# Two transformer blocks on one core: the value products of block 2's three attention branches with the operands exchanged, heads in column halves

## The chip, the cores and the metric

One core of one Trainium2 chip runs the whole program. The metric is the time of one execution on the device in microseconds (us). Before the change three runs gave a median of 1591.19 us (1590.44 to 1591.41).

## The reference, cut to what matters

Batch 1, 256 tokens, width 1024, all in float32. Two different block types, each two layers deep, run one after the other. Only the second is changed:

```
for l in range(2):                                # second_block
    h = rms_norm_2(x, g_mix[l]);  proj = h @ w_in[l]
    y_a = mla_mixer(...)            # 8 heads, keys of 96, values of 64, full 256 x 256 softmax
    y_b = dilated_mixer(...)        # 4 head places x 3 dilation groups, values of 64; the three
                                    # groups are joined by a softmax over their log-sums
    y_c = neighbourhood_mixer(...)  # 8 heads, keys and values of 64, a window with a bias
    merged = gates0 * (y_a @ w_pa) + gates1 * (y_b @ w_pb) + gates2 * (y_c @ w_pc)
    x = x + merged @ w_o[l]
    h = rms_norm_2(x, g_ffn[l])
    x = x + (silu(h @ w1[l]) * (h @ w3[l])) @ w2[l]
```

Each branch is softmax(scores) times values for each head. In branch b the three groups of one head place share one softmax: the exponentials of all three, divided by their common sum, times their values, summed.

## The kernel before, in words

**Weights.** All weight matrices are cut into 252 pieces of up to 128 x 2048 floats, loaded in a fixed order into a ring of three buffers (`raw`), one DMA each from SyncE (SP). ScalarE rounds a piece to a high half (`split_high`, L895, `wh`), VectorE makes the low half (`split_low`, L1251, `wl`), and TensorE multiplies high by high, high by low and low by high (L404, L405, L406). A piece of full width is 24 such matmuls. Piece q+3 reuses the buffer of piece q. The pieces of a layer of block 2 are numbered 0 to 74; pieces 12, 13, 32 and 33 are half as wide as the others here (`NARROW`).

**Attention in steps.** Every engine has one list of instructions, written out by hand in this order, and all run in program order with semaphores between them. The attention of a layer is 24 steps, m = 0 to 23, beside pieces q = 11 + m: steps 0 to 7 are branch a, 8 to 15 branch b, 16 to 23 branch c (`step_kind`); within a branch four steps (j = 0 to 3) for each half t of the 256 queries. A step of a or c is two heads, a step of b is one head place with its three groups (768 keys). In each step TensorE does, after the matmuls of piece q: the value product of step m-1 (`weighted`, L796 or L802), the transposes of step m's probabilities (`probs_t`, by the helper at L442), and the scores of step m+1 (`scores`: L752 for a, L770 for b, L758 for c). The 128 queries' probabilities lie in `prob` with queries on partitions; their transpose `prob_t` has keys on partitions.

**The value product** takes 128 x 128 of `prob_t` as the stationary operand and 128 x 64 of the values as the moving one, so its output has queries on partitions and heads along the row. The exponentials of the softmax go in undivided. After the last step of a branch half, `output` (L1703) takes the reciprocal of the sums (L1710) and scales all heads at once from PSUM into `y` (L1711). The products with w_pb, w_pa and w_pc (pieces 32 and up) need y with its columns on partitions, so y is transposed on TensorE: branch b after step 17, branch a after steps 19 and 20, branch c in the middle of piece 35 (`branch_c_t`, L812). VectorE copies the transposes to `xf` (L1260), ScalarE makes the high half (L900), VectorE the low half (L1270).

**VectorE in a step**: copy the transposed probabilities out of PSUM (L1375), `output` where a half has ended, the row maxima of step m+1 (`row_max`; L1699, L1680 or L1694, then L1683 or L1700), and `split_low` of piece q+2 (L1770). From step 21 on a product of a gate (`merge`, L1722) comes first. **ScalarE in a step**: copies or gates out of PSUM (L929, L1177), `split_high` of piece q+3 (L1179), the exponentials of step m+1 (`softmax_exp`, L1142 or L1149). Half-array matmuls are already there in the scores of b and c, whose 64-row operands lie on partitions 0 to 63 or 64 to 127.

Of the kernel before, what the change touches and what calls it, by code (L numbers as in the profile page):

```python
# [76 lines left out]
    "tr_full": (24, 69), "tr_free": (24, 69), "xh_ready": (12, 19), "xl_ready": (12, 19),  # L77
# [9 lines left out]
    "s_full": (0, STEPS), "max_ready": (0, STEPS), "p_ready": (0, STEPS),  # L87
    "o_full": (0, 6), "o_free": (0, 6), "bias_in": (0, 256), "bias_ready": (0, 1), "merged_ready": (0, 2), "sum_ready": (0, 2),
    "dve_step": (52, 81), "act_step": (6, 0),
# [72 lines left out]
def block2_transposes():  # L162
    order = [("norm1", 4), ("a", 2), ("bq", 2), ("bqk", 1), ("aq", 4), ("bk", 2), ("ak", 1),
             ("bk_last", 1), ("ak_rest", 3)]
    for m in range(STEPS):
        order.append((("pt", m), 2 if 8 <= m < 16 else 1))
        order += {5: [("cq", 2)], 7: [("ck", 2)], 17: [("yb", 1)], 19: [("ya", 1)],
                  20: [("ya_last", 1)]}.get(m, [])
    order += [("yc", 2), ("m0", 2), ("m1", 2), ("norm2", 4)]
# [11 lines left out]
def build(nc, weights, x_in, gains1, gains2, g_mid, g_final, consts, masks, rpb, out):  # L181
    ctx = ExitStack()
    with ctx:
# [85 lines left out]


# [17 lines left out]
        s_full, max_ready, p_ready = S["s_full"], S["max_ready"], S["p_ready"]  # L288
        o_full, o_free = S["o_full"], S["o_free"]
# [58 lines left out]
        def step_kind(m):  # L348
            return "abc"[m // 8], (m % 8) // 4, m % 4

# [47 lines left out]
        def _(pe):  # L398
# [287 lines left out]
            for layer in range(DEPTH):  # L686
# [87 lines left out]
                def probs_t(m):  # L774
                    n = TR2["pt", m]
                    pe.wait_ge(*p_ready.by(L, m + 1))
# [5 lines left out]
                def weighted(m):  # L782

                    kind, t, j = step_kind(m)
                    pe.wait_ge(*tr_free.by(L, TR2["pt", m] + (2 if kind == "b" else 1)))
                    if j == 0:
                        pe.wait_ge(*o_free.by(L, max(0, m // 4 - 1)))
# [4 lines left out]
                    if kind == "b":  # L792
                        for b in range(6):
                            g, s = group_order(j)[b // 2], b % 2
                            h = 4 * g + j
                            mm = nc.tensor.matmul(o[:, j * 64:(j + 1) * 64], prob_t[:, b * P:(b + 1) * P],  # L796
                                                  bv[:, s, h * 64:(h + 1) * 64], start=b == 0, stop=b == 5)
                    else:
                        v = av if kind == "a" else cv
                        for b in range(4):  # L800
                            h, s = 2 * j + b // 2, b % 2
                            mm = nc.tensor.matmul(o[:, h * 64:(h + 1) * 64], prob_t[:, b * P:(b + 1) * P],  # L802
                                                  v[:, s, h * 64:(h + 1) * 64], start=s == 0, stop=s == 1)
# [7 lines left out]

                def branch_c_t():  # L812
                    pe.wait_ge(*o_free.by(L, 6))
                    for b in range(2):
# [1158 lines left out]
```

## Time and profile before

| what | value |
|---|---|
| median of three runs | 1591.19 us |
| the profiled execution, its own time | 1590.36 us |
| its span, first to last instruction | 1588.5 us |
| TensorE (PE) busy | 1567.9 us, 99% |
| PE weight loads (PEld) | 1304.7 us, 82% |
| VectorE (DVE) busy | 1037.2 us, 65% |
| ScalarE (ACT) busy | 769.4 us, 48% |
| GpSimd (POOL) busy | 39.8 us, 3% |

The busy times are unions of instruction spans. PE and PEld are two views of one engine: a matmul record and the weight load that goes with it. The ends of matmul records are modelled, so the distance from one start to the next tells more than a record's length. A f32 matmul that isn't a transpose leaves two records; a transpose or a matmul of the rounded halves leaves one. Block 2's first layer takes its 24 steps from about 702 to 878 us, its second some 474 us later.

### The profile page before, as it was taken

The numbers are of one execution on the slowest core, as the hardware profiler recorded it, in microseconds if no ns is written. First come the engines' busy times: TensorE is split into PE (matmuls) and PEld (weight loads), VectorE is DVE, ScalarE is ACT, GpSimd is POOL, SyncE is SP. The second block draws the span as 40 slices with busy tenths as digits, with TensorE's granted clock in tenths as the row PEclk, the third lists the DMA queues.
The fourth block names the chain that finished last, engine by engine and source line by source line (L and its number), as shares of the span: only waits on it lengthen the run. The fifth ranks groups of instructions, "written<-read, shape, count | busy, mean of one in ns | idle before, by whom it ended". The sixth has DMA issues, their size and how long they took to land.

```text
span 1588.5 us, 18655 instructions
## 1 busy us (share of the span) xinstructions
PE 1567.9 (99%) x7684; PEld 1304.7 (82%) x7684; DVE 1037.2 (65%) x1309; ACT 769.4 (48%) x891; POOL 39.8 (3%) x28
## 2 busy tenths in 40 slices
PE   7999999999999999999999999999999999999997
PEld 5888888888888888888888888888888888888886
DVE  4778656666875656965556875656865547776555
ACT  5655444456454444664445354444664444454443
POOL 0000000001000000000020100000000020100000
PEclk9999999999999999999999999999999999999999
DMA  8435555554355554443543455554543633555551
GB/s 298 175 109 189 196 188 191 178 186 159 108 210 186 185 188 150 165 157 133 143 137 131 163 209 185 185 189 152 185 136 131 160 132 123 186 204 193 183 195 55
DMA packets 54243, 267.23 MB, mean 168 GB/s; under 512 B 18704, under 2 KB 19344, under 8 KB 24208
## 3 DMA queue, kind: packets, MB, share of 16 engines
q1 hardware_dynamic: 40784, 262.02, 46.5%
q10 hardware_dynamic: 13376, 4.02, 1.9%
q8 instruction: 61, 1.00, 0.3%
q14 instruction: 22, 0.18, 0.0%
HBM read 264.98 MB, written 1.05 MB: 167 GB/s over the span
## 4 chain that ended last, share of the span: by engine, by line
PE 93%; DVE 4%; ACT 1%; DMA 1%; issue 1%; SPq 0%; DVEq 0%; ACTq 0%
PE psum L404 27%; PE psum L406 27%; PE psum L405 26%; PE psum L442 4%; PE psum L802 2%; PE psum L796 1%; PE psum L496 1%; PE psum L770 1%; DMA raw<-in_weights 1%; PE psum L752 1%; DVE wl L1251 1%; PE psum L758 1%; PE psum L614 0%; PE psum L598 0%; ACT wh L895 0%
## 5 line engine op out<-in xcount | busy, mean ns | idle before, releaser
L1251 DVE TENSOR_TENSOR wl<-raw,wh 128x2048 fp32r<-128x2048 f32 (+1 forms) x250 | 560.8, 2246 | 276.6 <-ACT wh L895 273.6
L895 ACT ACTIVATE wh<-raw 128x2048 fp32r<-128x2048 f32 (+1 forms) x250 | 467.1, 1873 | 398.1 <-PE psum L406 384.0
L404 PE MATMUL psum<-wh,xh 128*128 128x512 f32 (+1 forms) x1632 | 647.4, 397 | 8.8 <-ACT work L929 3.7
L406 PE MATMUL psum<-wh,xl 128*128 128x512 f32 (+1 forms) x1632 | 633.1, 388 | 0.0
L405 PE MATMUL psum<-wl,xh 128*128 128x512 f32 (+1 forms) x1632 | 632.0, 387 | 0.0
L404 PEld LDWEIGHTS psum<-wh,xh 128*128 128x128 f32 x1632 | 307.1, 188 | 78.0 <-issue 15.9
L406 PEld LDWEIGHTS psum<-wh,xl 128*128 128x128 f32 x1632 | 306.8, 188 | 63.2
L405 PEld LDWEIGHTS psum<-wl,xh 128*128 128x128 f32 x1632 | 307.5, 188 | 57.6
L1375 DVE COPY arena<-psum 128x512 f32<-128x512 f32 x100 | 61.9, 643 | 159.6 <-PE psum L442 144.9
L404 PE MATMUL psum<-wh,ah 128*128 128x512 f32 (+1 forms) x360 | 140.3, 390 | 0.0
L406 PE MATMUL psum<-wh,al 128*128 128x512 f32 (+1 forms) x360 | 139.4, 387 | 0.0
L405 PE MATMUL psum<-wl,ah 128*128 128x512 f32 (+1 forms) x360 | 139.3, 387 | 0.0
L943 ACT ACTIVATE work<-psum,rms 128x256 f32<-128x256 f32 x88 | 41.7, 474 | 127.0 <-PE psum L406 127.0
L404 PEld LDWEIGHTS psum<-wh,ah 128*128 128x128 f32 x360 | 67.6, 188 | 13.7 <-issue 0.7
L406 PEld LDWEIGHTS psum<-wh,al 128*128 128x128 f32 x360 | 67.6, 188 | 13.5
L405 PEld LDWEIGHTS psum<-wl,ah 128*128 128x128 f32 x360 | 67.6, 188 | 13.1
L900 ACT ACTIVATE xh<-xf 128x512 fp32r<-128x512 f32 x56 | 34.3, 630 | 75.2 <-DVE xf L1264 50.1
L1390 DVE TENSOR_SCALAR work<-psum,rms 128x256 f32<-128x256 f32 x88 | 42.1, 479 | 28.7 <-ACT work L943 28.7
L929 ACT ACTIVATE work<-psum,rms 128x512 f32<-128x512 f32 (+2 forms) x52 | 32.9, 638 | 41.0 <-PE psum L406 41.0
L1392 DVE SCALAR_TENSOR_TENSOR work<-psum,rms,work 128x256 f32<-128x256 f32 x88 | 42.6, 484 | 3.1
L1841 POOL TENSOR_TENSOR arena<-arena,col_mask 128x768 f32<-128x768 f32 x8 | 18.5, 2350 | 789.4 <-DMA arena<-in_rpb 789.4
L1270 DVE TENSOR_TENSOR xl<-xf,xh 128x512 fp32r<-128x512 f32 x56 | 36.5, 688 | 2.2
(159 smaller groups left out, 1054.7 us busy)
## 6 DMA issues: line engine op xcount, KB each, us to landing
raw<-in_weights SPq DMA_DIRECT2D x234, 1024.0 KB, 4.8
raw<-in_weights SPq DMA_DIRECT2D x10, 512.0 KB, 3.6
raw<-in_weights SPq DMA_DIRECT2D x4, 832.0 KB, 4.3
arena<-in_rpb ACTq DMA_DIRECT2D x32, 96.0 KB, 8.1
raw<-in_weights SPq DMA_DIRECT2D x8, 256.0 KB, 6.8
raw<-in_weights SPq DMA_DIRECT2D x2, 768.0 KB, 4.5
x<-in_x SPq DMA_DIRECT2D x4, 256.0 KB, 4.5
out<-arena SPq DMA_DIRECT2D x3, 256.0 KB, 3.1
```

What stands on the lines that cost most here:

```text
L404: nc.tensor.matmul(dst, lh, right(wh, slot), start=start, stop=False)
L405: nc.tensor.matmul(dst, lh, right(wl, slot), start=False, stop=False)
L406: return nc.tensor.matmul(dst, ll, right(wh, slot), start=False, stop=stop)
L442: mm = nc.tensor.transpose(psum[0:w, TR + n % 2, col:col + P], src, ident[:, :])
L895: nc.scalar.activation(wh[:, slot, 0:n], raw[:, slot, 0:n], ACT.Copy).then_inc(high_ready.sem, 1)
L900: nc.scalar.activation(dst, part(xf[:, n % 2, :], 0, nk, SEQ), ACT.Copy)\
L943: nc.scalar.activation(mlp_tanh[:, t, :], bank(PROJ + t)[:, 0:256], ACT.Tanh, scale=rms[:, 6 + t:7 + t]).then_inc(tanh_ready.sem, 1)
L1251: nc.vector.tensor_tensor(wl[:, slot, 0:n], raw[:, slot, 0:n], wh[:, slot, 0:n].bitcast(F32), ALU.subtract).then_inc(split_ready.sem, 1)
L1270: nc.vector.tensor_tensor(low, part(xf[:, n % 2, :], 0, nk, SEQ), high.bitcast(F32), ALU.subtract).then_inc(xl_ready.sem, 1)
L1375: nc.vector.tensor_copy(dst, src).then_inc(tr_free.sem, 1)
L1390: step.wait(L, nc.vector.tensor_scalar(mlp_gate[:, t, :], bank(PROJ + t)[:, 0:256], rms[:, t:t + 1], None, ALU.mult))
L1392: nc.vector.scalar_tensor_tensor(mlp_act[:, t, :], bank(PROJ + t)[:, 256:512], rms[:, 6 + t:7 + t], mlp_gate[:, t, :], ALU.mult, ALU.mult) ...
```

## The change

The value products of all three branches exchange their operands: the values (128 keys x 64) are stationary and the transposed probabilities (128 keys x 128 queries) move, so the output has the 64 value columns on partitions and queries along the row, which is y transposed. Two heads go to partitions 0 to 63 and 64 to 127 of the output, and their matmuls alternate. Branch b has one head place in a step, so the product of an even step is left to the odd one after it, where both steps' twelve products alternate; the odd step's transposed probabilities go to `xf` for that. Since a query's sum now lies along the row, the probabilities are divided before they are transposed (`unit_sums` on VectorE, with the new semaphore `unit_ready`, on which TensorE's transposes wait in place of `p_ready`). `output` only halves and copies, into `y_t`, views of `y` with columns on partitions. The transposes of y, their copies to `xf` and the waits on them go; high and low halves are made from `y_t`. The output of the first half of branch c goes to ScalarE at step 20. VectorE's splits change places: in steps 1, 21 and 22 `unit_sums` stands ahead of them, and splits 33 and 34 each come a step earlier. Left out of the diff below: numbers of semaphore counts (five transposes fewer, 18 more ordered VectorE steps in a layer), and the declaration of the semaphore.

```diff
@@ -267,6 +266,9 @@
+        y_flat = y[:, :, :].rearrange("p a b -> p (a b)")
+        y_t = {"a": part(y_flat, 0, 4, SEQ), "b": part(y_flat, 1024, 2, SEQ), "c": part(y_flat, 1536, 4, SEQ)}
+
...
@@ -347,6 +350,11 @@
             return "abc"[m // 8], (m % 8) // 4, m % 4
+
+        def transposed(m):
+
+            kind, _, j = step_kind(m)
+            return xf[:, :, :].rearrange("p a b -> p (a b)") if kind == "b" and j % 2 else prob_t
...
@@ -773,7 +781,7 @@
                     n = TR2["pt", m]
-                    pe.wait_ge(*p_ready.by(L, m + 1))
+                    pe.wait_ge(*unit_ready.by(L, m + 1))
                     blocks = 6 if step_kind(m)[0] == "b" else 4
...
@@ -782,8 +790,10 @@
                     kind, t, j = step_kind(m)
+                    if kind == "b" and j % 2 == 0:
+                        return
                     pe.wait_ge(*tr_free.by(L, TR2["pt", m] + (2 if kind == "b" else 1)))
-                    if j == 0:
+                    if j == (1 if kind == "b" else 0):
                         pe.wait_ge(*o_free.by(L, max(0, m // 4 - 1)))
...
@@ -791,16 +801,23 @@
                         for b in range(6):
-                            g, s = group_order(j)[b // 2], b % 2
-                            h = 4 * g + j
-                            mm = nc.tensor.matmul(o[:, j * 64:(j + 1) * 64], prob_t[:, b * P:(b + 1) * P],
-                                                  bv[:, s, h * 64:(h + 1) * 64], start=b == 0, stop=b == 5)
+                            for step in (m - 1, m):
+                                jj = step % 4
+                                g, s = group_order(jj)[b // 2], b % 2
+                                h = 4 * g + jj
+                                mm = nc.tensor.matmul(o[64 * (jj % 2):64 * (jj % 2) + 64, (j // 2) * P:(j // 2 + 1) * P],
+                                                      bv[:, s, h * 64:(h + 1) * 64],
+                                                      transposed(step)[:, b * P:(b + 1) * P],
+                                                      start=b == 0, stop=b == 5)
                     else:
                         v = av if kind == "a" else cv
-                        for b in range(4):
-                            h, s = 2 * j + b // 2, b % 2
-                            mm = nc.tensor.matmul(o[:, h * 64:(h + 1) * 64], prob_t[:, b * P:(b + 1) * P],
-                                                  v[:, s, h * 64:(h + 1) * 64], start=s == 0, stop=s == 1)
+                        for s in range(2):
+                            for hh in range(2):
+                                h = 2 * j + hh
+                                mm = nc.tensor.matmul(o[64 * hh:64 * hh + 64, j * P:(j + 1) * P],
+                                                      v[:, s, h * 64:(h + 1) * 64],
+                                                      prob_t[:, (2 * hh + s) * P:(2 * hh + s + 1) * P],
+                                                      start=s == 0, stop=s == 1)
                     if j == 3:
...
@@ -808,12 +825,6 @@
-
-                def branch_c_t():
-                    pe.wait_ge(*o_free.by(L, 6))
-                    for b in range(2):
-                        transpose_k(L, TR2["yc"] + b, lambda t, k: y[:, t, k * P:(k + 1) * P],
-                                    (6 + 2 * b, 7 + 2 * b))
...
@@ -853,15 +864,8 @@
                         staged_t(TR2["ck"], 0)
-                    if m == 17:
-                        pe.wait_ge(*o_free.by(L, 4))
-                        transpose_k(L, TR2["yb"], lambda t, k: y[:, t, k * P:(k + 1) * P], (4, 5))
-                    if m == 19:
-                        transpose_k(L, TR2["ya"], lambda t, k: y[:, t, k * P:(k + 1) * P], (0, 1))
-                    if m == 20:
-                        transpose_k(L, TR2["ya_last"], lambda t, k: y[:, t, k * P:(k + 1) * P], (2, 3))
                 weighted(STEPS - 1)
-                project(L, 35, 22, 0, between=branch_c_t)
+                project(L, 35, 22, 0)
...
@@ -869,7 +873,8 @@
-                project(L, 36, 23, 4, left_ready=9)
+                pe.wait_ge(*xl_ready.by(L, 11))
+                project(L, 36, 23, 4)
                 project(L, 37, 24, 4, between=lambda: merged(0))
...
@@ -1152,6 +1157,13 @@
+                def branch_c_high(t):
+
+                    act.wait_ge(*used(L, 31))
+                    act.wait_ge(*o_free.by(L, 5 + t))
+                    tq = slice(t * P, (t + 1) * P)
+                    nc.scalar.activation(xh[:, 4:8, tq], y_t["c"][:, :, tq], ACT.Copy).then_inc(xh_ready.sem, 1)
+
                 softmax_exp(0)
...
@@ -1177,14 +1189,24 @@
                     split_high(L, q + 3)
+                    if m == 20:
+                        act.wait_ge(*o_full.by(L, 5))
+                        nc.scalar.activation(y_t["c"][:, :, 0:P], part(bank(ACC + 2), 0, 4, P), ACT.Copy, scale=0.5)\
+                            .then_inc(o_free.sem, 1)
                     if m + 1 < STEPS:
...
                     if m == 17:
-                        operand_high(L, 6, TR2["yb"], dst=ah[:, 0:2, :])
+                        act.wait_ge(*used(L, 9))
+                        act.wait_ge(*o_free.by(L, 4))
+                        nc.scalar.activation(ah[:, 0:2, :], y_t["b"], ACT.Copy).then_inc(xh_ready.sem, 1)
                     if m == 19:
-                        operand_high(L, 7, TR2["ya"], dst=xh[:, 0:2, :])
-                    if m == 20:
-                        operand_high(L, 8, TR2["ya_last"], dst=xh[:, 2:4, :])
+                        act.wait_ge(*used(L, 30))
+                        act.wait_ge(*o_free.by(L, 2))
+                        for k in (0, 2):
+                            nc.scalar.activation(xh[:, k:k + 2, :], y_t["a"][:, k:k + 2, :], ACT.Copy)\
+                                .then_inc(xh_ready.sem, 1)
+                    if m == 21:
+                        branch_c_high(0)
                     if 8 <= m < 12:
...
@@ -1196,8 +1218,7 @@
                                 .then_inc(bias_in.sem, 16)
-                for b in range(2):
-                    operand_high(L, 9 + b, TR2["yc"] + b, dst=xh[:, 4 + 2 * b:6 + 2 * b, :])
+                branch_c_high(1)
                 split_high(L, 38)
...
@@ -1700,19 +1721,32 @@
+                def unit_sums(m):
+
+                    kind, t, j = step_kind(m)
+                    v.wait_ge(*p_ready.by(L, m + 1))
+                    heads = [prob] if kind == "b" else [prob[:, 0:SEQ], prob[:, SEQ:2 * SEQ]]
+                    at = 32 + 4 * t + j if kind == "b" else (0 if kind == "a" else 16) + 8 * t + 2 * j
+                    step.wait(L, nc.vector.reciprocal(rden[:, 0:len(heads)], den[:, at:at + len(heads)]))
+                    for hh, p in enumerate(heads):
+                        ins = nc.vector.tensor_scalar(p, p, rden[:, hh:hh + 1], None, ALU.mult)
+                    ins.then_inc(unit_ready.sem, 1)
+
                 def output(i):
...
                     kind, t = "abc"[i // 2], i % 2
-                    heads = 4 if kind == "b" else 8
-                    at = {"a": 0, "b": 32, "c": 16}[kind] + heads * t
-                    to = {"a": 0, "b": 512, "c": 768}[kind]
+                    k = 2 if kind == "b" else 4
                     v.wait_ge(*o_full.by(L, i + 1))
-                    step.wait(L, nc.vector.reciprocal(rden[:, 0:heads], den[:, at:at + heads]))
-                    nc.vector.scalar_tensor_tensor(
-                        y[:, t, to:to + heads * 64].rearrange("p (h e) -> p h e", e=64),
-                        part(bank(ACC + 2 + t), 0, heads, 64), 0.5,
-                        rden[:, 0:heads].unsqueeze(2).to_broadcast([P, heads, 64]), ALU.mult, ALU.mult)\
-                        .then_inc(o_free.sem, 1)
+                    nc.vector.tensor_scalar(y_t[kind][:, :, t * P:(t + 1) * P], part(bank(ACC + 2 + t), 0, k, P),
+                                            0.5, None, ALU.mult).then_inc(o_free.sem, 1)
+
+                def branch_low(n, src, high, low):
+                    v.wait_ge(*xh_ready.by(L, n + 1))
+                    nc.vector.tensor_tensor(low, src, high.bitcast(F32), ALU.subtract).then_inc(xl_ready.sem, 1)
+
+                def branch_c_low(t):
+                    tq = slice(t * P, (t + 1) * P)
+                    branch_low(9 + t, y_t["c"][:, :, tq], xh[:, 4:8, tq], xl[:, 4:8, tq])
...
@@ -1733,14 +1767,15 @@
+                unit_sums(0)
...
-                        copy_t(L, n, prob_t[:, 0:512], others=m == 0)
+                        copy_t(L, n, transposed(m)[:, 0:512], others=m == 0)
...
-                            copy_t(L, n + 1, prob_t[:, 512:768])
+                            copy_t(L, n + 1, transposed(m)[:, 512:768])
...
@@ -1752,7 +1787,7 @@
-                    if m >= 1 and (m - 1) % 4 == 3:
+                    if m >= 1 and (m - 1) % 4 == 3 and m != 20:
...
@@ -1761,25 +1796,23 @@
                                        c_t[:, first + 2 * b:first + 2 * b + 2, :])
+                        if m in (1, 21, 22):
+                            unit_sums(m + 1)
+                            if m != 21:
+                                split_low(L, 14 if m == 1 else 35)
+                        else:
+                            split_low(L, 34 if m == 20 else q + 2)
+                            unit_sums(m + 1)
                         if m == 17:
-                            operand_out(L, 6, TR2["yb"], None)
+                            branch_low(6, y_t["b"], ah[:, 0:2, :], al[:, 0:2, :])
                         if m == 19:
-                            operand_out(L, 7, TR2["ya"], None)
-                        if m == 20:
-                            operand_out(L, 8, TR2["ya_last"], None)
-                        split_low(L, q + 2)
-                        if m == 17:
-                            operand_low(L, 6, ah[:, 0:2, :], al[:, 0:2, :])
-                        if m == 19:
-                            operand_low(L, 7, xh[:, 0:2, :], xl[:, 0:2, :])
-                        if m == 20:
-                            operand_low(L, 8, xh[:, 2:4, :], xl[:, 2:4, :])
+                            for k in (0, 2):
+                                branch_low(7 + k // 2, y_t["a"][:, k:k + 2, :], xh[:, k:k + 2, :], xl[:, k:k + 2, :])
+                            split_low(L, 33)
                 output(5)
-
-                def branch_c():
-                    operand(L, 9, TR2["yc"], 4, None, 2)
-
-                merge(35, 0, 1, 23, between=branch_c)
+                branch_c_low(0)
+
+                merge(35, 0, 1, 23, between=lambda: branch_c_low(1))
                 split_low(L, 37)
```

## Rows read from the trace of the kernel before

**Rows 1.** The page: busy time by engine; shares of the chain that ended last.

```profile
PE 1567.9 (99%) x7684; PEld 1304.7 (82%) x7684; DVE 1037.2 (65%) x1309; ACT 769.4 (48%) x891; POOL 39.8 (3%) x28
...
PE 93%; DVE 4%; ACT 1%; DMA 1%; issue 1%; SPq 0%; DVEq 0%; ACTq 0%
```

**Rows 2.** Timeline of TensorE, last product and y's transposes: start, length, line, operands, count.

```profile
876.82 0.39 PE L406 MATMUL psum<-wh,xl 128*128 128x512 f32 x1
...
878.17 0.39 PE L405 MATMUL psum<-wl,xh 128*128 128x512 f32 x1
...
880.48 0.39 PE L406 MATMUL psum<-wh,xl 128*128 128x512 f32 x1
...
881.82 0.40 PE L405 MATMUL psum<-wl,xh 128*128 128x512 f32 x1
```

**Rows 3.** The same view in block 1: f32 streams with 128 and 256 moving columns.

```profile
87.79 0.39 PE L617 MATMUL psum<-arena 128*128 128x128 f32 x2
...
89.35 1.89 PE L598 MATMUL psum<-arena 128*128 128x256 f32 x8
91.08 1.05 PE L603 MATMUL psum<-arena 128*128 128x128 f32 x8
```

**Rows 4.** The same view around step 3, branch a.

```profile
725.12 0.39 PE L406 MATMUL psum<-wh,xl 128*128 128x512 f32 x1
...
727.72 0.40 PE L405 MATMUL psum<-wl,xh 128*128 128x512 f32 x1
```

**Rows 5.** The same view around step 10, branch b.

```profile
774.57 0.39 PE L406 MATMUL psum<-wh,xl 128*128 128x512 f32 x1
...
776.84 1.13 PE L770 MATMUL psum<-arena 64*128 64x256 f32 x6
...
778.23 0.39 PE L405 MATMUL psum<-wl,xh 128*128 128x512 f32 x1
```

**Rows 6.** The same view around step 18, branch c.

```profile
842.22 0.39 PE L406 MATMUL psum<-wh,xl 128*128 128x512 f32 x1
...
843.82 0.70 PE L758 MATMUL psum<-arena 64*128 64x256 f32 x4
...
844.79 0.39 PE L405 MATMUL psum<-wl,xh 128*128 128x512 f32 x1
```

**Rows 7.** Groups by line and shape: busy us, mean ns, idle before.

```profile
L1817 DVE TENSOR_SCALAR arena<-arena,rms 128x512 f32<-128x512 f32 x3 | 1.3, 483 | 0.0
...
L1658 DVE TENSOR_SCALAR work<-work,rms 128x256 f32<-128x256 f32 x4 | 1.2, 351 | 0.1
```

**Rows 8.** Timelines of VectorE and TensorE, step 8 to 9.

```profile
762.22 2.28 DVE L1251 TENSOR_TENSOR wl<-raw,wh 128x2048 fp32r<-128x2048 f32 x1
...
765.90 0.39 PE L406 MATMUL psum<-wh,xl 128*128 128x512 f32 x1
```

**Rows 9.** Timelines of VectorE, ScalarE and TensorE, steps 1 and 2.

```profile
708.24 2.28 DVE L1251 TENSOR_TENSOR wl<-raw,wh 128x2048 fp32r<-128x2048 f32 x1
...
709.18 0.20 ACT L1149 ACTIVATION_READ_ACCUMULATOR arena<-psum,smax 128x1 f32 x1
...
712.50 0.40 PE L405 MATMUL psum<-wl,xh 128*128 128x512 f32 x1
```

**Rows 10.** The same views, steps 20 and 21.

```profile
858.85 0.61 PE L442 MATMUL psum<-ident,arena 128*128 128x128 f32 x4
...
858.80 1.90 ACT L895 ACTIVATE wh<-raw 128x2048 fp32r<-128x2048 f32 x1
...
860.33 0.69 DVE L1711 SCALAR_TENSOR_TENSOR y<-psum,rden 128x512 f32<-128x512 f32 x1
...
861.82 0.69 DVE L1260 COPY xf<-psum 128x512 f32<-128x512 f32 x1
...
864.12 0.61 PE L442 MATMUL psum<-ident,arena 128*128 128x128 f32 x4
```

More of the change, by code:

```diff
@@ L76 @@
     "acc_full": (5, 5), "x_ready": (8, 8),
-    "tr_full": (24, 69), "tr_free": (24, 69), "xh_ready": (12, 19), "xl_ready": (12, 19),
+    "tr_full": (24, 64), "tr_free": (24, 64), "xh_ready": (12, 19), "xl_ready": (12, 19),
     "sumsq_ready": (4, 3), "var_ready": (4, 3), "root_ready": (4, 3), "rms_ready": (2, 3),
@@ L86 @@
     "aq_ready": (0, 1), "ak_ready": (0, 1),
-    "s_full": (0, STEPS), "max_ready": (0, STEPS), "p_ready": (0, STEPS),
+    "s_full": (0, STEPS), "max_ready": (0, STEPS), "p_ready": (0, STEPS), "unit_ready": (0, STEPS),
     "o_full": (0, 6), "o_free": (0, 6), "bias_in": (0, 256), "bias_ready": (0, 1), "merged_ready": (0, 2), "sum_ready": (0, 2),
-    "dve_step": (52, 81), "act_step": (6, 0),
+    "dve_step": (52, 99), "act_step": (6, 0),
 }
@@ L166, in block2_transposes @@
         order.append((("pt", m), 2 if 8 <= m < 16 else 1))
-        order += {5: [("cq", 2)], 7: [("ck", 2)], 17: [("yb", 1)], 19: [("ya", 1)],
-                  20: [("ya_last", 1)]}.get(m, [])
-    order += [("yc", 2), ("m0", 2), ("m1", 2), ("norm2", 4)]
+        order += {5: [("cq", 2)], 7: [("ck", 2)]}.get(m, [])
+    order += [("m0", 2), ("m1", 2), ("norm2", 4)]
     at, where = 0, {}
@@ L288, in build @@
         s_full, max_ready, p_ready = S["s_full"], S["max_ready"], S["p_ready"]
+        unit_ready = S["unit_ready"]
         o_full, o_free = S["o_full"], S["o_free"]
```

## The prediction

> **What bounds the kernel now.** I read the page's busy line and its chain first: TensorE has work for 1567.9 of 1588.5 us, and 93% of the chain that ended last is TensorE [rows 1]. So an edit in block 2's attention is worth what it changes in the stream of matrix records, plus any moment in which that stream newly waits. The view for both is the timeline of TensorE around one of the 24 steps, with those of VectorE and ScalarE beside it.
>
> How I price a step: take the start of the last L406 record of a weight piece and the start of the first L405 record after the step, and subtract two normal spacings of 0.23 us (that L406's own and the L404's between them). What is left is what the step inserts. Done on the lone last product of the layer, eight records insert 878.17 - 876.82 = 1.35 less 0.46, so 0.89 us, 0.111 a record; eight transposes of y insert 881.82 - 880.48 = 1.34 less 0.46, 0.88 us, 0.11 each [rows 2]. A f32 matmul leaves two records, so a step of branch a or c has 8 product records and one of b has 12. Inside a stream of f32 records with 128 moving columns the spacing is (89.35 - 87.79) / 14 = 0.111 us, and with 256 columns (91.08 - 89.35) / 8 = 0.216 [rows 3]. So a product with 64 moving columns costs the same as one with 128: turning it round (v stationary with 64 columns, probabilities moving with 128) does not by itself cost more.
>
> A step of branch a inserts 2.60 - 0.46 = 2.14 us [rows 4]; 8 + 4 records at 0.11 and the four 256-column score records at 0.216 give 2.18. Nothing is left over. A step of b inserts 3.66 - 0.46 = 3.20 [rows 5]: 12 + 6 records are 1.98; its six score records work on half the rows each, and two pairs of them run beside each other, so they take four places, 0.86; 0.36 is left. A step of c inserts 2.57 - 0.46 = 2.11 [rows 6]: 1.32 for twelve, 0.43 for two places of paired records, and again 0.36 is left. So going into half-array matmuls and back costs about 0.36 us a time, and pairs on two halves do run at the same time: four score records in two places.
> The Trainium skill says the same of the price: "TensorEngine Tiling (Array Packing)", Key Properties, has it that changing the tiling mode drains the engine. By that rule the column halves of the change pay it too; the 96-row scores of branch a don't, and rows 4 agree.
>
> **The change, part by part** (both layers together; 32 steps of a and c, 8 pairs of b steps).
> 1. *Products of a and c.* Before: 8 x 0.11 = 0.88 us. After: the two heads go to column halves, four places of 0.112 if they run together, plus a way in and out: 0.45 + 0.36 = 0.81. Gain 0.07 x 32 = 2.2 us. No row shows column halves. Bounds of one place: 0.108 (the stream of 128 columns, half of 0.216) and 0.223 (one after the other). Bounds of the way in and out: 0 (as in branch a) to about 0.6 if leaving fp32r work for column halves costs more than rows 5 and 6 show. I take 0.112 and 0.36, since the row halves in the same kernel, same data type, are the nearest rows.
> 2. *Products of b.* Before: 24 x 0.11 = 2.64 us for two steps. After: one way in and out for both and twelve places: 1.34 + 0.36 = 1.70. Gain 0.94 x 8 = 7.5 us.
> 3. *Transposes of y.* 20 a layer go (yb 4, ya 4, ya_last 4, yc 8): 40 x 0.11 = 4.4 us, all in TensorE's stream. The copies behind them go from VectorE too.
> 4. *unit_sums.* VectorE now divides the probabilities before they are transposed: a reciprocal and two 256-column scales, or one of 768. Rows: 0.351 us for 256 columns and 0.483 for 512, SBUF to SBUF with a scalar from a column [rows 7]; the same line to 768 gives 0.62. With 0.2 for the reciprocal and the wait, 0.85 us a step, some 40 us in all on an engine that is busy 1037 of 1588 us. It is on TensorE's path only where it ends after TensorE is ready to transpose. In a full step of b it starts at the end of the split, 762.22 + 2.28 = 764.50, and ends at 765.35, while the piece ends at 765.90 + 0.23 = 766.13 [rows 8]: hidden, with 0.8 us to spare, and that is the tightest kind (an odd b step, with no product ahead of the transposes). Full steps of a and c have the products to spare as well. If the cover went, each step would pay its lateness once.
>  Two places are tighter. (i) Step m=1 puts unit_sums(2) before split_low(14): ScalarE's exponentials end at 709.38, the scales at 710.2, and the split, 2.28 us, at 712.45; TensorE wanted piece 14 at 712.50 - 0.23 = 712.27, and now 0.14 earlier after two cheaper products [rows 9]. It waits about 0.4 us. (ii) The narrow pieces 32 and 33. The transposes of step 20 now start 0.5 us earlier, 858.35 instead of 858.85. The row maxima of step 21 ended 861.82 - 858.85 = 2.97 us after them, with the output of branch c (0.9 us) between; that output goes to ScalarE, so it is 2.1 and VectorE is free at 860.5 (ScalarE's split of piece 34 ends at 860.2 at the latest, so that is no later). Then split_low(34), 2.28, and unit_sums(21), 0.85: 863.6. TensorE wants to transpose at 864.12 - 0.9 = 863.2, having lost two groups of transposes and some of two products [rows 10]: 0.4 us late. Steps 22 and 23 come out level by the same counting (VectorE: two gate products, copy, maxima, scales; ScalarE: exponentials), within 0.2 us. Together about 1.0 us a layer, 2.0 in all; bounds 0 and 6 (each of steps 21, 22, 23 late by 0.6 as well).
> 5. *Moved.* Output 4 to ScalarE before its exponentials of step 21 (0.7 us, inside the 2 us in which it waits for the maxima); the high and low halves of y come straight from SBUF instead of over xf, earlier than before; splits 33 and 34 run a step earlier, so SP's loads of pieces 36 and 37 start earlier, split 35 and with it the load of 38 about a microsecond later with several to spare. Branch c's last operand is still made during piece 35, 5.5 us long, and needs about 3. I cost all of it at nothing, for that cover.
>
> Sum: -2.2 - 7.5 - 4.4 + 2.0 = -12.1. The profiled execution took 1590.36 us, so 1578.3; the median of the runs, 1591.19, is 0.83 above it, so 1579.1.
>
> A rule of the skill speaks against this: "TensorE: Matmul & The Clock Gate", Part 3, says that a weight load overlaps a running matmul only where the row groups differ, and column halves share all rows. In this trace full-array products reload 128 rows and columns every 0.111 us beside the stream, so loads do hide behind matmuls of the same rows; the rule is therefore not taken as it stands, but it is what the next two rivals would be.
>
> **Rivals.**
> - *A, the halves take turns* (slower). Each column half has its load and its stream one after the other, 0.111 a record. Then a and c: 0.89 + 0.36 = 1.25, +0.37 x 32 = +11.8; b: 2.66 + 0.36 = 3.02, +0.38 x 8 = +3.0; transposes -4.4; waits about +1 since TensorE comes later. +11.4: 1602.6. It decides from a place of 0.17 us upward. For: no row shows column halves, and the spacing of 0.111 at 64 as at 128 moving columns says that loads are what bounds these records. Against: the loads get half as wide, and row halves run in pairs.
> - *B, half hidden*: a pair takes 0.167, one 64-column load (half of 0.111) beyond the stream. a and c: 0.67 + 0.36 = 1.03, +0.15 x 32 = +4.8; b: 2.00 + 0.36 = 2.36, -0.28 x 8 = -2.2; -4.4 + 2.0: +0.2, 1591.4, no change.
> - *C, VectorE late*: halves overlap, but the scales end late in steps 1 and 21 to 23, 6 us in all: 1583.1. For: steps 22 and 23 are within 0.2 us; against: all other steps have 0.8 us or more.
> - *D, no price for column halves*: 0.36 x 40 = 14.4 more, of which some 3 turn into waits for VectorE: 1567.7. For: branch a's 96 rows pay none; against: both kinds of half-array matmul here do.
>
> **How the numbers follow.** My forecast 0.50, A 0.18, B 0.14, C 0.12, D 0.06. A measurement of this kernel can tell 0.2%, 3.2 us, from no change. Forecast, C and D are faster, 0.68; B splits into 0.05 faster, 0.05 same, 0.04 slower; A is slower. So 0.73, 0.05, 0.22. The range leaves out A and D: 1571 (a cheaper way in and out, no new waits) to 1594 (B with its own error, or a way in and out of 0.7 us instead of 0.36, which alone would add 14 us).
>
> **What would show it.** In the profile after: product records that start in pairs a few ns apart, and an insert of about 2.1 us for an a step with 0.8 of it for the products (A would show records 0.111 apart; B pairs 0.167 apart); an idle of TensorE's weight queue of about 0.2 us at the way in and again at the way out; one long group of 24 records in every second b step, 1.3 us; no transposes of y in block 2; waits of TensorE on VectorE's scales at steps 1 and 21 of each layer, under 0.6 us, and none in the other steps. The forecast is wrong if column halves don't pair, or if the scales are waited for in every step.

## The result and the profile after

Four runs of the changed kernel gave a median of 1579.91 us (1579.04 to 1580.84) against 1591.30 for the kernel before on the same chip: a ratio of 0.9928, 95% interval 0.9916 to 0.9940. The forecast was 1579.1 us. The profiled execution took 1579.04 us, 11.3 less than the one before, where the sum said 12.1.

The page of the changed kernel, lines that answer to [rows 1]:

```profile
PE 1555.5 (99%) x7644; PEld 1272.9 (81%) x7644; DVE 1068.8 (68%) x1413; ACT 769.0 (49%) x893; POOL 40.1 (3%) x28
...
PE 89%; DVE 7%; ACT 2%; DMA 1%; issue 1%; SPq 0%; DVEq 0%; ACTq 0%
```

Forty matmul records fewer (the transposes of y), 104 VectorE instructions more, and TensorE's share of the chain down from 93% to 89%: VectorE now ends some waits. In the changed kernel L412, L413 and L414 are the former L404 to L406, L450 the former L442; the products are L808 (branch b) and L817 (a and c), the scales of `unit_sums` L1732 (the reciprocal before it L1730), the split L1272, `output` L1740, the low halves of y L1745, GpSimd's sum of gates L1881.

The timeline of TensorE around step 3, branch a, which answers to [rows 4], and the same stretch of its weight queue (PEld):

```profile
725.72 0.39 PE L414 MATMUL psum<-wh,xl 128*128 128x512 f32 x1
726.04 0.66 PE L817 MATMUL psum<-arena 128*64 128x128 f32 x8
726.63 0.66 PE L450 MATMUL psum<-ident,arena 128*128 128x128 f32 x4
...
728.22 0.39 PE L413 MATMUL psum<-wl,xh 128*128 128x512 f32 x1
```

```profile
726.04 0.42 PEld L817 LDWEIGHTS psum<-arena 128*64 128x64 f32 x8 [0.35 <-issue]
726.62 0.42 PEld L450 LDWEIGHTS psum<-ident,arena 128*128 128x128 f32 x4 [0.17 <-issue]
```

By the measure of the prediction the step inserts 728.22 - 725.72 - 0.46 = 2.04 us instead of 2.14. The weight queue is idle before the first load of the column halves and again before the first full-array load behind them: that is the way in and out. The product of the pair of b steps 8 and 9, which TensorE makes in its step 10, in the first of the two views; it answers to [rows 5]. Here operands tell the halves apart, `arena` for the even step's probabilities and `xf` for the odd one's:

```profile
773.33 0.39 PE L414 MATMUL psum<-wh,xl 128*128 128x512 f32 x1
773.64 0.32 PE L808 MATMUL psum<-arena 128*64 128x128 f32 x1
773.65 0.32 PE L808 MATMUL psum<-xf,arena 128*64 128x128 f32 x1
773.80 0.27 PE L808 MATMUL psum<-arena 128*64 128x128 f32 x1
773.81 0.27 PE L808 MATMUL psum<-xf,arena 128*64 128x128 f32 x1
773.91 0.27 PE L808 MATMUL psum<-arena 128*64 128x128 f32 x1
...
774.90 0.27 PE L808 MATMUL psum<-xf,arena 128*64 128x128 f32 x1
775.11 0.87 PE L450 MATMUL psum<-ident,arena 128*128 128x128 f32 x6
```

The records start in twos, 0.01 us apart, and the twos follow every 0.11 us. Twelve places for 24 records.

In this attention TensorE now waits at three places of each layer: at piece 14 (VectorE's split, late behind the scales), behind the product of step 20 (VectorE's scales L1732 in front of the transposes) and at piece 36. The timeline of TensorE there, first layer:

```profile
712.89 0.50 PE L412 MATMUL psum<-wh,xh 128*128 128x512 f32 x1 [0.18 <-DVE wl L1272]
...
857.99 0.66 PE L817 MATMUL psum<-arena 128*64 128x128 f32 x8
859.11 0.66 PE L450 MATMUL psum<-ident,arena 128*128 128x128 f32 x4 [0.47 <-DVE arena L1732]
...
878.86 0.50 PE L412 MATMUL psum<-wh,xh 128*128 128x512 f32 x1 [0.52 <-DVE xl L1745]
```

The bracket at piece 14 understates that wait: the step before it inserts 2.38 us, and 1.94 where the scales are left out (below). The third wait wasn't forecast. VectorE's timeline before it, then GpSimd's:

```profile
874.49 0.69 DVE L1740 TENSOR_SCALAR y<-psum 128x512 f32<-128x512 f32 x1
875.09 2.52 DVE L1745 TENSOR_TENSOR xl<-y,xh 128x512 fp32r<-128x512 f32 x1
877.53 0.67 DVE L1756 SCALAR_TENSOR_TENSOR work<-work,psum 128x512 f32<-128x512 f32 x1
878.13 0.68 DVE L1745 TENSOR_TENSOR xl<-y,xh 128x512 fp32r<-128x512 f32 x1
```

```profile
874.65 2.40 POOL L1881 TENSOR_TENSOR work<-work 128x1024 f32<-128x1024 f32 x1 [67.22 <-DVE work L1756]
```

The same subtraction takes 0.68 us the second time and 2.52 the first, while GpSimd's sum of gates runs from 874.65 to 877.05. The instruction ends 0.56 us after GpSimd does, as if it had only begun then. TensorE starts piece 36 about 0.8 us late for it, in each layer.

GpSimd also works beside the scales once in each layer, in its additions on `arena` at branch b. VectorE's timeline and GpSimd's, first layer:

```profile
801.92 3.82 DVE L1272 TENSOR_TENSOR wl<-raw,wh 128x2048 fp32r<-128x2048 f32 x1
...
805.85 2.00 DVE L1732 TENSOR_SCALAR arena<-arena,rden 128x768 f32<-128x768 f32 x1
```

```profile
798.15 9.28 POOL L1874 TENSOR_TENSOR arena<-arena,col_mask 128x768 f32<-128x768 f32 x4 [406.64 <-DMA arena<-in_rpb]
```

The split takes 3.82 us instead of 2.28 there and the scale 2.00 instead of 0.62, although the scale reads only one large operand. The cover holds even so: that pair of b steps inserts 0.04 us more than the others.

### The profile page after: what moved, and what is told of

It is laid out like the page before. It is cut to its first block, busy times and chain, and to the rows that moved or that the text cites. A ratio compares the mean times of both kernels' runs of the same rounds, so it can differ in the third digit from the quotient of the medians.

```text
span 1577.3 us, 18675 instructions
## 1 busy us (share of the span) xinstructions
PE 1555.5 (99%) x7644; PEld 1272.9 (81%) x7644; DVE 1068.8 (68%) x1413; ACT 769.0 (49%) x893; POOL 40.1 (3%) x28
## 4 chain that ended last, share of the span: by engine, by line
PE 89%; DVE 7%; ACT 2%; DMA 1%; issue 1%; SPq 0%; DVEq 0%; ACTq 0%
PE psum L412 26%; PE psum L414 26%; PE psum L413 26%; PE psum L450 4%; DVE wl L1272 2%; PE psum L504 1%; PE psum L778 1%; DMA raw<-in_weights 1%; PE psum L817 1%; PE psum L760 1%; PE psum L808 1%; DVE work L1756 1%; ACT wh L900 0%; PE psum L622 0%; PE psum L606 0%
## 5 line engine op out<-in xcount | busy, mean ns | idle before, releaser
L1272 DVE TENSOR_TENSOR wl<-raw,wh 128x2048 fp32r<-128x2048 f32 (+1 forms) x250 | 561.8, 2250 | 277.1 <-ACT wh L900 274.1
L412 PE MATMUL psum<-wh,xh 128*128 128x512 f32 (+1 forms) x1632 | 647.8, 397 | 9.0 <-ACT work L934 3.0
L414 PE MATMUL psum<-wh,xl 128*128 128x512 f32 (+1 forms) x1632 | 633.3, 388 | 0.0
L413 PE MATMUL psum<-wl,xh 128*128 128x512 f32 (+1 forms) x1632 | 632.5, 388 | 0.0
L412 PEld LDWEIGHTS psum<-wh,xh 128*128 128x128 f32 x1632 | 307.3, 188 | 81.7 <-issue 16.8
L414 PEld LDWEIGHTS psum<-wh,xl 128*128 128x128 f32 x1632 | 307.2, 188 | 63.2
L413 PEld LDWEIGHTS psum<-wl,xh 128*128 128x128 f32 x1632 | 307.8, 189 | 57.4
L412 PE MATMUL psum<-wh,ah 128*128 128x512 f32 (+1 forms) x360 | 140.4, 390 | 0.0
L414 PE MATMUL psum<-wh,al 128*128 128x512 f32 (+1 forms) x360 | 139.3, 387 | 0.0
L413 PE MATMUL psum<-wl,ah 128*128 128x512 f32 (+1 forms) x360 | 139.2, 387 | 0.0
L1396 DVE COPY arena<-psum 128x512 f32<-128x512 f32 x84 | 53.7, 661 | 94.7 <-PE psum L450 83.9
L412 PEld LDWEIGHTS psum<-wh,ah 128*128 128x128 f32 x360 | 67.6, 188 | 14.4 <-issue 1.3
L414 PEld LDWEIGHTS psum<-wh,al 128*128 128x128 f32 x360 | 67.6, 188 | 13.5
L413 PEld LDWEIGHTS psum<-wl,ah 128*128 128x128 f32 x360 | 67.6, 188 | 13.1
L905 ACT ACTIVATE xh<-xf 128x512 fp32r<-128x512 f32 x48 | 29.4, 631 | 69.4 <-DVE xf L1285 50.6
L450 PEld LDWEIGHTS psum<-ident,work 128*128 128x128 f32 (+1 forms) x252 | 29.1, 136 | 8.1 <-issue 2.0
```

Source lines behind the costliest of these rows:

```text
L412: nc.tensor.matmul(dst, lh, right(wh, slot), start=start, stop=False)
L413: nc.tensor.matmul(dst, lh, right(wl, slot), start=False, stop=False)
L414: return nc.tensor.matmul(dst, ll, right(wh, slot), start=False, stop=stop)
L450: mm = nc.tensor.transpose(psum[0:w, TR + n % 2, col:col + P], src, ident[:, :])
L905: nc.scalar.activation(dst, part(xf[:, n % 2, :], 0, nk, SEQ), ACT.Copy)\
L1272: nc.vector.tensor_tensor(wl[:, slot, 0:n], raw[:, slot, 0:n], wh[:, slot, 0:n].bitcast(F32), ALU.subtract).then_inc(split_ready.sem, 1)
```

## The experiments

Each is an edit of the changed kernel. Ratios are to the kernel before on the same chip as the run (1592.13 us for the first four edits, 1592.06 for the others). Beside the time, the table gives a length that leaves out the noise of block 1: in the profiled execution, from the first score record of branch a in block 2 to the last matmul record (before: 693.21 to 1580.00). It rests on one execution each: in some of them a wait of TensorE for one of ScalarE's gates (0.17 to 0.53 us) turns up that others don't have, so a difference of half a microsecond has to be traced to its rows.

| kernel | median us (runs) | ratio to before, 95% interval | that length, us |
|---|---|---|---|
| before | 1591.3 (4) | | 886.8 |
| the change | 1579.91 (4) | 0.9928, 0.9916 to 0.9940 | 875.0 |
| halves in turn | 1587.85 (10) | 0.9974, 0.9964 to 0.9984 | 882.8 |
| full array in a and c | 1584.00 (4) | 0.9950, 0.9935 to 0.9965 | 878.9 |
| no scales | 1577.43 (4) | 0.9907, 0.9892 to 0.9922 | 872.0 |
| sum later | 1578.24 (4) | 0.9916, 0.9902 to 0.9931 | 873.7 |
| pairs in all branches | 1576.98 (4) | 0.9905, 0.9889 to 0.9922 | 871.9 |
| pairs, and sum later | 1575.84 (4) | 0.9902, 0.9887 to 0.9916 | 871.6 |
| b in blocks of 2 | 1580.98 (1) | | 875.7 |
| b in blocks of 3 | 1581.96 (1) | | 877.2 |

**Halves in turn.**

```diff
-                        for b in range(6):
-                            for step in (m - 1, m):
+                        for step in (m - 1, m):
+                            for b in range(6):
...
-                        for s in range(2):
-                            for hh in range(2):
+                        for hh in range(2):
+                            for s in range(2):
```

> The changed kernel, except that the matmuls of one column half all come before those of the other (branches a and c: head by head; branch b: step by step), so neighbours in the stream use the same half. Same matmuls, same number of ways in and out. Theory (column halves gain because neighbouring matmuls on different halves run side by side): a record takes 0.111 us instead of half a place, so a and c steps insert 2.05 + 0.45 us and a pair of b steps 3.52 + 1.3; 32 x 0.45 + 8 x 1.3 = +25 us against the changed kernel, so about 1604. Rival (the gain comes from stationary operands of half the width, which load faster, or the engine pairs them in any order): the product stays at 0.6 to 0.7 us and the time at 1580.

Measured: 7.8 us slower in the trace, not 25. A step of a inserts 2.05 us (2.04 before the edit), a step of c 2.00 as before: there the order doesn't matter. A pair of b steps inserts 4.44 instead of 3.52, and 8 x 0.92 = 7.4 is nearly all of the loss. TensorE's timeline of a pair of b steps:

```profile
773.90 1.20 PE L808 MATMUL psum<-arena 128*64 128x128 f32 x9
774.83 0.32 PE L808 MATMUL psum<-xf,arena 128*64 128x128 f32 x1
774.93 0.27 PE L808 MATMUL psum<-arena 128*64 128x128 f32 x1
774.99 0.27 PE L808 MATMUL psum<-xf,arena 128*64 128x128 f32 x1
775.04 0.27 PE L808 MATMUL psum<-arena 128*64 128x128 f32 x1
775.10 0.27 PE L808 MATMUL psum<-xf,arena 128*64 128x128 f32 x1
775.15 0.27 PE L808 MATMUL psum<-arena 128*64 128x128 f32 x1
775.21 1.15 PE L808 MATMUL psum<-xf,arena 128*64 128x128 f32 x9
```

Neither theory holds as it was put. One half alone runs a record in 0.109 us, against 0.111 for the full array, so half-width weights make next to nothing faster; but neighbours need not alternate either. The second half's first record starts beside the ninth of twelve, with three of the first half's records still ahead of it. So TensorE starts work of an idle half out of the program's order, some four records early, and four records of a head in a and c are within that reach. The Trainium skill, "TensorE: Matmul & The Clock Gate", Part 3, says that matmuls start strictly in program order; these rows contradict it. New theory: a look-ahead of four records. Two runs put it to the test.

**Blocks of 2 and of 3 matmuls in branch b.** The edit for blocks of 2; the other has 3 in place of each 2.

```diff
-                        for b in range(6):
-                            for step in (m - 1, m):
+                        for b0 in range(0, 6, 2):
+                            for step, b in [(step, b) for step in (m - 1, m) for b in range(b0, b0 + 2)]:
```

> The changed kernel with branch b's products in blocks: two matmuls (four records) of one step's half, then two of the other's, and so on. Theory (TensorE starts a record of the idle half when the running half is at most four records ahead of it in order, as the run with the halves in turn showed: the second half began beside the ninth of twelve): full overlap as when alternating, a pair of b steps inserts 3.5 us. Rival (only neighbours overlap): 3.5 + about 0.6 to 1.1.

> The same in blocks of three matmuls (six records). Theory (look-ahead of four records): the idle half starts beside the third record of a block, two places lost in all, a pair of b steps inserts 3.5 + 0.22 = 3.7 us. Rival (look-ahead of eight records or of time, not of order): 3.5.

Each was run once, so the times don't rank them; the inserts of all eight pairs in a trace can be compared. Measured: 3.57 us a pair in blocks of 2 (in two places more, 3.64 and 3.78), 3.79 in blocks of 3, against 3.52. In blocks of 2 the second half starts 0.01 us after the first. In blocks of 3, TensorE's timeline shows the second half starting beside the third record, 774.35 + 2 x 0.11 and a little:

```profile
774.35 0.54 PE L808 MATMUL psum<-arena 128*64 128x128 f32 x3
774.62 0.32 PE L808 MATMUL psum<-xf,arena 128*64 128x128 f32 x1
...
775.60 0.27 PE L808 MATMUL psum<-arena 128*64 128x128 f32 x1
775.66 0.49 PE L808 MATMUL psum<-xf,arena 128*64 128x128 f32 x3
```

The start is where the new theory puts it, to 0.05 us, and the inserts are 0.07 us over what it said (3.5 and 3.72). Whether the reach is four records or a number of instructions that holds four of them, these runs don't tell.

**Full array in a and c.**

```diff
-                                mm = nc.tensor.matmul(o[64 * hh:64 * hh + 64, j * P:(j + 1) * P],
-                                                      v[:, s, h * 64:(h + 1) * 64],
+                                mm = nc.tensor.matmul(o[:, j * P:(j + 1) * P],
+                                                      v[:, s, 2 * j * 64:(2 * j + 2) * 64],
...
-                                                      start=s == 0, stop=s == 1)
+                                                      start=(s, hh) == (0, 0), stop=(s, hh) == (1, 1))
```

> The changed kernel, except that in branches a and c both heads' values are stationary together (128 columns, full array) for each head's probabilities, and all four matmuls of a step add into one output: the heads are mixed, so the outputs of a and c are left wrong. Eight records of the full array, no way in or out of column halves. Theory (a way in and out costs 0.36 us and eats nearly all that the pairing gives in a step of two heads): 0.88 us for a product instead of 0.77 measured in the changed kernel, +0.11 x 32 = +3.5 us, about 1583.5, and no idle of the weight queue around the product. Rival (the idle shown there is no cost, only how records are drawn): 0.88 against 0.45, +0.43 x 32 = +14 us, 1594.

Measured: +3.9 us in the trace. TensorE's timeline around step 3 of branch a:

```profile
725.97 0.39 PE L414 MATMUL psum<-wh,xl 128*128 128x512 f32 x1
726.20 1.05 PE L817 MATMUL psum<-arena 128*128 128x128 f32 x8
...
728.62 0.40 PE L413 MATMUL psum<-wl,xh 128*128 128x512 f32 x1
```

The weight queue has no idle around it. The lone last product inserts 0.89 us, and 0.79 in the changed kernel. Pairs take 4 x 0.109 = 0.44 of that, so the way in and out is 0.35. The rival is out: it would have shown +14. A step of a inserts 2.65 - 0.46 = 2.19 us here against 2.04 with column halves and 2.14 in the kernel before, a step of c 2.16 against 2.00 and 2.11. So in branches a and c the column halves gain about 0.15 us a step over the full array, and turning the product round without them costs 0.05. Where TensorE waits for VectorE anyway (piece 14, step 21, half of the wait at piece 36), the longer product costs nothing, which is why the whole is 3.9 and not 32 x 0.15 = 4.8.

**No scales.**

```diff
-                    step.wait(L, nc.vector.reciprocal(rden[:, 0:len(heads)], den[:, at:at + len(heads)]))
-                    for hh, p in enumerate(heads):
-                        ins = nc.vector.tensor_scalar(p, p, rden[:, hh:hh + 1], None, ALU.mult)
-                    ins.then_inc(unit_ready.sem, 1)
+                    nc.vector.reciprocal(rden[:, 0:len(heads)], den[:, at:at + len(heads)])\
+                        .then_inc(unit_ready.sem, 1)
```

> The changed kernel without the division: VectorE only takes the reciprocal and signals, the probabilities are left undivided, so the output is wrong. Theory (some 42 us of new work on VectorE costs only where TensorE waits for it, 0.5 us at step 21 and 0.4 at piece 14 of each layer): -1.9 us, 1578. Rival 1 (VectorE's load also delays the splits and loads over the whole stretch, or slows ScalarE): more than -4 us. Rival 2 (the waits are of other origin): 0.

Measured: -3.0 us in the trace. The step before piece 14 inserts 1.94 instead of 2.38 us, the one with step 21's transposes 2.00 instead of 2.53: together 0.97 a layer. The wait of 0.8 us at piece 36, which the expectation left out, is gone as well: without the scales VectorE ends the last low half 6.0 us after the last product starts, not 6.8, though the long subtraction is still there (2.50 us). That would be -3.5; one pair of b steps in the first layer gives 0.6 back, where TensorE waits 0.53 us for a gate of ScalarE (L1189), at 795.01. So 32.4 us of scales on VectorE cost 2 to 3 us of time.

**Sum later.**

```diff
+                    if n == 0:
+                        pool.wait_ge(*xl_ready.by(L, 11))
```

> The changed kernel, except that GpSimd's first sum of gates waits until the last low half of branch c is done (xl_ready 11) before it starts. Theory (VectorE's subtraction for branch c's first low half took 2.5 us instead of 0.69 because GpSimd was adding at the same time, and that is why TensorE waits 1.0 us at piece 36 of each layer): the subtraction back at 0.69, the wait gone, -2.0 us, about 1578. Rival (it was slow for another reason, ScalarE's copy beside it): the subtraction stays above 2 us and the time at 1580; or the collision moves to the split that follows and delays piece 38, then +0 to +1.

Measured: -1.3 us in the trace. The group of L1745 `xl<-y,xh` runs from 679 to 687 ns, none at 2.5 us, and no wait at piece 36 is left. VectorE's and GpSimd's timelines:

```profile
875.28 0.68 DVE L1745 TENSOR_TENSOR xl<-y,xh 128x512 fp32r<-128x512 f32 x1
...
879.18 2.68 DVE L1272 TENSOR_TENSOR wl<-raw,wh 128x2048 fp32r<-128x2048 f32 x1
```

```profile
877.31 2.40 POOL L1883 TENSOR_TENSOR work<-work 128x1024 f32<-128x1024 f32 x1 [69.78 <-DVE xl L1745]
```

The sum now meets a gate product with one operand in PSUM at 878.58, which takes 0.69 us, and only the end of it meets a split, which takes 2.68 instead of 2.28. The gain is 1.3 us instead of the 2.0 expected, since the wait was 0.8 a layer and not 1.0, and the transposes that follow piece 36 insert 0.97 us instead of 0.88. By the medians alone it couldn't be told from the changed kernel; the rows show it. The Trainium skill, "SBUF — State Buffer", "Who interferes with whom", says that GpSimd and a VectorE operation with two SBUF inputs lock each other out for a whole instruction; the 2.52 us agree, and so does the untouched PSUM operand.

**Pairs in all branches.** `weighted` returns for every even j, `transposed` gives `xf` for every odd one, the waits for free buffers move to the odd steps, and the product of a and c loops over both steps. The second kernel has the edit of *sum later* besides.

```diff
-                        for s in range(2):
-                            for hh in range(2):
-                                h = 2 * j + hh
...
+                        for step in (m - 1, m):
+                            jj = step % 4
+                            for s in range(2):
+                                for hh in range(2):
+                                    h = 2 * jj + hh
```

> The changed kernel with branches a and c done as branch b: the product of an even step waits for the odd one (its probabilities in the other buffer), so two steps share one way in and out of the column halves. Theory (that way costs 0.33 us, measured as 0.77 us for eight records in pairs, less four places of 0.109): 16 pairs x 0.33 = -5.3 us, the wait for piece 14 gone, -0.9, but the transposes of odd steps follow straight on a piece and wait for VectorE's scales at steps 1, 21 and 23, some +0.25, +0.6 and +0.35 a layer: together -3.7 against the changed kernel, about 1576. Rival (the waits take all of it, since VectorE's order was set for single steps): 1580 or more, with over 2.5 us of waits a layer on the scales.

> The previous kernel, with GpSimd's first sum of gates held back until branch c's last low half is done. Theory (the two edits don't meet): the wait of 1.0 us at piece 36 of each layer goes here too, another -2.0 us, about 1574.3 and the fastest of all. Rival (the later product of steps 22 and 23 makes output and low halves the last again): no difference to the kernel without it.

Measured: -3.1 and -3.4 us in the trace. Two steps of a insert 1.31 + 2.48 = 3.79 us instead of 4.08: 0.3 for each pair saved, where 0.33 was priced. But step 21's transposes follow straight on piece 32 now and wait for the scales. TensorE's timeline of the first, then VectorE's:

```profile
857.35 0.39 PE L414 MATMUL psum<-wh,al 128*128 128x512 f32 x1
858.80 0.66 PE L450 MATMUL psum<-ident,arena 128*128 128x128 f32 x4 [1.06 <-DVE arena L1734]
```

```profile
855.73 2.28 DVE L1274 TENSOR_TENSOR wl<-raw,wh 128x2048 fp32r<-128x2048 f32 x1
857.93 0.16 DVE L1732 RECIPROCAL rden<-den 128x2 f32<-128x2 f32 x1
858.13 0.62 DVE L1734 TENSOR_SCALAR arena<-arena,rden 128x256 f32<-128x256 f32 x2
```

That is 1.3 us a layer where 0.6 on top of 0.5 was expected. The sum held back removes the wait at piece 36 here too, but its expectation missed: -0.3 us against the kernel without it, not -2.0. With pairs everywhere that wait was down to 0.5 us a layer. Of the 1.0 so gained, 0.2 is lost at the transposes behind piece 36, and 0.5 in one wait for a gate of ScalarE (0.49 us at 776.52) that the other trace doesn't have.

This last kernel has the lowest median, 1575.84 us, 16.2 below the kernel before on its chip. Its interval only touches that of the change, so it is faster than the change by the traces and the medians together; from the one without the later sum no run tells it apart.

## Why the prediction was right

By the steps of the prediction, all from the traces.

1. *Products of a and c*: forecast -2.2; a step of a fell from 2.14 to 2.04 us, one of c from 2.11 to 2.00, so about 0.105 x 32 = -3.4. This term was mis-sized. A step without a product inserts 1.31 us (pairs in all branches), so the product of a fell from 0.83 to 0.73, not from 0.88 to 0.81. The old one was cheaper than counted where transposes follow it: "does not by itself cost more" holds for the lone product only, elsewhere turning costs 0.05, as the full-array run showed. The new one was cheaper still: a place is 0.109 and the way in and out 0.29 in a step (0.35 at the lone product), where I took 0.112 and 0.36.
2. *Products of b*: forecast -7.5; two steps inserted 3.20 each, 6.40 us, before and 1.91 + 3.52 = 5.43 after: -0.97 x 8 = -7.8.
3. *Transposes of y*: forecast -4.4; three groups of 0.39 and one of 0.88 a layer, -4.1.
4. *Waits on the scales*: forecast +2.0; 0.44 at piece 14 and 0.53 at step 21 a layer, +1.9, both at the places named. Scales took 0.351 and, undisturbed, 0.62 us, the numbers taken.
5. *Moved work*: forecast 0; this is the step that failed, in its sentence that branch c's last operand "needs about 3" of piece 35's 5.5 us. From the output's start to the end of the last low half it took 878.81 - 874.49 = 4.3 us, since GpSimd's sum stood beside the first subtraction, and VectorE, busy with a split and a gate product, came to the output only 1.9 us after piece 35 had begun: +0.8 a layer, +1.6. With the sum later the same start is early enough, and the wait is gone.

-3.4 - 7.8 - 4.1 + 1.9 + 1.6 = -11.8, which is the difference in the length of the table; between the two executions it was 11.3. The term that failed was covered by the first one, mis-sized the other way. That is luck: the total is nearer than its parts.

Rivals: A and B fell with the first pair of records, C with the transposes of steps 22 and 23, which wait for nothing, D with the lone product's 0.79 us, where four places alone are 0.44, and with the full-array run. The assumption that decided it was that column halves behave as the row halves in the scores do.

## What to carry to other kernels

Price a step by what it inserts between two records of a steady stream, not by the lengths of its records; with that, the row halves already in a trace gave the price of a product on column halves to about a tenth (0.81 us forecast, 0.73 and 0.79 measured; 1.70 forecast and 1.60 for two b steps). A way in and out of half-array matmuls cost about a third of a microsecond here, so gather work of one kind: eight f32 records gained 0.1 us, 24 almost a microsecond. When an edit adds or moves a VectorE operation whose operands all lie in SBUF, look at what GpSimd does at that moment as well.

## What the runs showed of the hardware

- Column halves of f32 matmuls (64 stationary columns, 128 moving) run side by side: a pair every 0.109 us. One half alone takes 0.109 a record.
- TensorE starts a record of an idle half ahead of up to three earlier ones of the busy half: beside the ninth of twelve, beside the third of six.
- The way into and out of column halves took 0.35 us between two pieces and 0.29 with transposes behind it; into and out of row halves it was 0.36 by the prediction's count.
- An f32 product of eight full-array records with 64 moving columns inserted 0.05 us less than one with 128 where transposes followed (2.14 against 2.19 a step), and the same 0.89 between two pieces.
- VectorE's subtraction of two SBUF operands went from 0.68 to 2.52 us beside a GpSimd addition of 2.40 us; a gate product with an operand in PSUM took 0.69 beside it, against 0.68 alone. A scale from SBUF to SBUF with 768 columns went from 0.62 to 2.00 us beside GpSimd's additions, and a split from 2.28 to 3.82.
